# A decoder trunk in split float32 on one core: the operands of each stage at distances of their own from a multiple of 2048 bytes

## The reference

```python
mem_n = rmsnorm(mem, mem_norm)
for i in range(2):
    x = x + 0.5 * swiglu_ffn(rmsnorm(x, ffn1_norm[i]), ffn1_w_in[i], ffn1_w_out[i])   # 1024 -> 2*2816 -> 1024
    h = rmsnorm(x, mix_norm[i])
    mk, mv = split(mem_n @ mem_w_kv[i])
    z = h @ w_in[i]                                # hgrn: 1024 -> 5120; gmlp: 1024 -> 5120
    x = x + concatenate([mixer(z), memory_attention(z, mk, mv)]) @ w_out[i]
    x = x + 0.5 * swiglu_ffn(rmsnorm(x, ffn2_norm[i]), ffn2_w_in[i], ffn2_w_out[i])
return rmsnorm(x, final_norm)
```

## Time and profile before

| | before |
|---|---|
| median of 3 runs | 2362.61 us (2361.79 to 2364.54) |
| profiled execution, its own time | 2362.44 us |
| its span | 2360.7 us |
| TensorE busy, matmuls | 2340.6 us, 99% |
| VectorE busy | 1197.9 us, 51% |
| ScalarE busy | 743.0 us, 31% |
| GpSimd busy | 263.3 us, 11% |
| mean DMA rate | 99 GB/s |

### The profile page before, as it was taken

One profiled execution on the slowest core, in us unless ns is written; L12 is line 12 of the kernel. 1 busy time (PEld: TensorE's weight loads), 2 busy tenths in 40 slices (PEclk: granted clock), 3 DMA queues, 4 the chain that ended last, 5 costly groups with the idle time before them and its releaser, 6 DMA issues.

```text
span 2360.7 us, 29488 instructions
## 1 busy us (share of the span) xinstructions
PE 2340.6 (99%) x10944; PEld 1943.6 (82%) x10944; DVE 1197.9 (51%) x1411; ACT 743.0 (31%) x1005; POOL 263.3 (11%) x235
## 2 busy tenths in 40 slices
PE   9999999999999999999999999999999999999998
PEld 9988888877888888888878888887788888888887
DVE  6654443446888654444445444344337644444422
ACT  4432222234444322222223223123333322322322
POOL 3400001111333420000110000120001212000000
PEclk9999999999999999999999999999999999999999
DMA  7733333332222333333333333333233233333322
GB/s 233 215 98 96 94 94 98 98 107 63 72 71 78 100 91 97 98 98 98 97 90 91 96 98 98 98 98 98 70 94 88 83 96 107 98 98 94 93 95 92
DMA packets 400691, 234.32 MB, mean 99 GB/s; under 512 B 7692, under 2 KB 386672, under 8 KB 400624
## 3 DMA queue, kind: packets, MB, share of 16 engines
q1 hardware_dynamic: 397328, 223.37, 32.1%
q0 software_dynamic: 3280, 10.02, 1.2%
q10 hardware_dynamic: 16, 0.00, 0.0%
HBM read 227.07 MB, written 6.29 MB: 99 GB/s over the span
## 4 chain that ended last, share of the span: by engine, by line
PE 95%; DVE 2%; ACT 1%; issue 1%; DMA 0%; POOL 0%; ACTq 0%; DVEq 0%; SPq 0%; POOLq 0%
PE acc L1012 26%; PE acc L1014 26%; PE acc L1013 26%; PE acc L766 1%; PE acc L768 1%; PE acc L767 1%; PE mix L398 1%; PE mix L385 1%; PE acc L249 1%; PE acc L251 1%; PE acc L250 1%; PE mix L250 1%; PE mix L249 1%; PE mix L251 1%; PE mix L833 1%
## 5 line engine op out<-in xcount | busy, mean ns | idle before, releaser
L1174 DVE TENSOR_TENSOR w_lo<-raw,w_hi 128x1024 fp32r<-128x1024 f32 (+1 forms) x422 | 548.3, 1302 | 658.4 <-ACT w_hi L1444 647.8
L1012 PE MATMUL acc<-h_hi,w_hi 128*128 128x512 f32 x1920 | 759.2, 395 | 7.5 <-DVE h_lo L1236 5.3
L1014 PE MATMUL acc<-h_hi,w_lo 128*128 128x512 f32 x1920 | 748.4, 390 | 0.0
L1013 PE MATMUL acc<-h_lo,w_hi 128*128 128x512 f32 x1920 | 747.9, 390 | 0.0
L1444 ACT ACTIVATE w_hi<-raw 128x1024 fp32r<-128x1024 f32 (+1 forms) x422 | 436.5, 1038 | 354.3 <-DMA raw<-in_ffn_w_out_dram 222.0
L1012 PEld LDWEIGHTS acc<-h_hi,w_hi 128*128 128x128 f32 x1920 | 361.3, 188 | 85.2 <-DVE h_lo L1236 6.6
L1013 PEld LDWEIGHTS acc<-h_lo,w_hi 128*128 128x128 f32 x1920 | 361.2, 188 | 77.0 <-issue 3.7
L1014 PEld LDWEIGHTS acc<-h_hi,w_lo 128*128 128x128 f32 x1920 | 360.9, 188 | 75.6
L1012 PE MATMUL acc<-act_hi,w_hi 128*128 128x512 f32 (+1 forms) x976 | 368.7, 378 | 2.6 <-DVE act_lo L1185 1.7
L1014 PE MATMUL acc<-act_hi,w_lo 128*128 128x512 f32 (+1 forms) x976 | 366.2, 375 | 0.0
L1013 PE MATMUL acc<-act_lo,w_hi 128*128 128x512 f32 (+1 forms) x976 | 366.1, 375 | 0.0
(11 more groups left out here) (214 smaller groups left out, 1779.0 us busy)
## 6 DMA issues: line engine op xcount, KB each, us to landing
raw<-in_ffn_w_in_dram SPq DMA_DIRECT2D x176, 512.0 KB, 3.7
raw<-in_ffn_w_out_dram SPq DMA_DIRECT2D x70, 512.0 KB, 4.0
raw<-in_hgrn_w_in_dram SPq DMA_DIRECT2D x40, 512.0 KB, 3.7
raw<-in_gmlp_w_in_dram SPq DMA_DIRECT2D x40, 512.0 KB, 3.6
raw<-in_mem_w_kv_dram SPq DMA_DIRECT2D x32, 512.0 KB, 4.2
raw<-in_gmlp_w_out_dram SPq DMA_DIRECT2D x24, 512.0 KB, 4.0
raw<-in_ffn_w_out_dram SPq DMA_DIRECT2D x24, 384.0 KB, 3.4
raw<-in_hgrn_w_out_dram SPq DMA_DIRECT2D x16, 512.0 KB, 4.0
```

The lines of the kernel that those rows point to most:

```text
L1012: pe.matmul(bank, w_hi[:, j, i, :], hi, start=(start and i == 0), stop=False)
L1013: pe.matmul(bank, w_hi[:, j, i, :], lo, start=False, stop=False)
L1014: m = pe.matmul(bank, w_lo[:, j, i, :], hi, start=False, stop=(stop and i == last))
L1174: dve.tensor_tensor(w_lo[:, j, 0:nkb], raw[:, j, 0:nkb], f32(w_hi[:, j, 0:nkb]), ALU.subtract).then_inc(w_lo_ready, 1)
```

## The change

The halves of h are now views of one tile, `h_flat`, with 2048 bytes to spare, and each `_in` stage s has two numbers of elements (4 bytes each) in `H_AT[s]`, by which its h_hi and h_lo begin behind a multiple of 2048 bytes: (512, 512), (0, 0), (64, 64), (0, 64), (1024, 1024), (128, 128) bytes for s = 0 to 5. The activations of the four feed-forward parts have `ACT_AT[n_ffn]`: (64, 64), (256, 256), (0, 1024), (0, 0) bytes; they use two spare blocks of act_hi and act_lo. The mixer's activations and the memory's halves stay where they were. act_hi, act_lo, work and vecs begin 2048 bytes later than before.

```diff
+H_ROOM = 512
+H_AT = [(128, 128), (0, 0), (16, 16), (0, 16), (256, 256), (32, 32)]
+ACT_AT = [(16, 16), (64, 64), (0, 256), (0, 0)]
...
-        with nc.sbuf_tensor("h_hi", [P, DB, T], F32R) as h_hi, nc.sbuf_tensor("h_lo", [P, DB, T], F32R) as h_lo:
+        with nc.sbuf_tensor("h_flat", [P, 2 * DB * T + H_ROOM], F32R) as h_flat:
             pass
-        out_rows = sb("out_rows", [P, 2 * DB, T])[:, 0:DB, :].rearrange("p b t -> p (b t)").rearrange(
-            "p (tb c) -> p tb c", tb=TB)
+        out_rows = sb("out_rows", [P, 2 * DB * T + H_ROOM])[:, 0:DB * T].rearrange("p (tb c) -> p tb c", tb=TB)
+
+        def h_views(s):
+
+            hi, lo = H_AT[s]
+            return [h_flat[:, at:at + DB * T].rearrange("p (b t) -> p b t", t=T) for at in (hi, DB * T + lo)]
...
+        def act_views(n):
+
+            hi, lo = ACT_AT[n]
+            return [part[:].rearrange("p b t -> p (b t)")[:, at:at + FB * T].rearrange("p (b t) -> p b t", t=T)
+                    for part, at in ((act_hi, hi), (act_lo, lo))]
...
-                unit(ph.q0 + it, j, h_parts, acc[j][:], True, True, each if first and j == 0 else None)
+                unit(ph.q0 + it, j, h_parts_of(s), acc[j][:], True, True, each if first and j == 0 else None)
...
+                    top, rest = act_views(n_ffn) if kind == "ffn_out" else (act_hi, act_lo)
...
-                            parts = [(act_hi[:, a0 + k, :], act_lo[:, a0 + k, :]) for k in range(nkb)]
+                            parts = [(top[:, a0 + k, :], rest[:, a0 + k, :]) for k in range(nkb)]
...
-                            dve.tensor_tensor(act_lo[:, f, :], tmp[:, j, :], f32(act_hi[:, f, :]),
+                            dve.tensor_tensor(rest[:, f, :], tmp[:, j, :], f32(top[:, f, :]),
...
-                act.activation(h_hi[:, m_, :], t, ACT.Copy).then_inc(h_hi_ready, 1)
+                act.activation(h_views(s)[0][:, m_, :], t, ACT.Copy).then_inc(h_hi_ready, 1)
```

More of the change, by code:

```diff
@@ L754, in v_tensor @@
                 pe.wait_ge(w_lo_ready, LANES * q + j + 1)
+                h_hi, h_lo = h_views(4)
                 top = w_hi[:, j].rearrange("p (k z) c -> p k (z c)", k=2)
@@ L1064, in _, with h_parts_of @@
                 (k_quad if kind == "k" else v_quad)(it)
-            h_parts = [(h_hi[:, k, :], h_lo[:, k, :]) for k in range(DB)]
+            def h_parts_of(s):
+                hi, lo = h_views(s)
+                return [(hi[:, k, :], lo[:, k, :]) for k in range(DB)]
             def in_unit(ph, s, it, j, first=False):
@@ L1119, in u_unit @@
                             pe.wait_ge(acc_read, ph.g0 + 2 * XH + LANES * it + j - 3)
-                        unit(ph.q0 + 6 + it, j, h_parts, acc[j][:], True, True)
+                        unit(ph.q0 + 6 + it, j, h_parts_of(s), acc[j][:], True, True)
                     for j in range(LANES):
@@ L1234, in h_rest @@
             def h_rest(s, m_, t):
+                h_hi, h_lo = h_views(s)
                 dve.wait_ge(h_hi_ready, DB * s + m_ + 1)
@@ L1305, in up, with low @@
                             dve.tensor_tensor(tmp[:, j, :], tmp[:, j, :], tmp[:, j - 1, :], ALU.mult).then_inc(prod_done, 1)
-                        def rest(j):
+                        def low(j):
                             f = 2 * it + j // 2
+                            top, rest = act_views(n_ffn)
                             dve.wait_ge(act_hi_ready, f0 + j // 2 + 1)
-                            dve.tensor_tensor(act_lo[:, f, :], tmp[:, j, :], f32(act_hi[:, f, :]),
+                            dve.tensor_tensor(rest[:, f, :], tmp[:, j, :], f32(top[:, f, :]),
                                               ALU.subtract).then_inc(act_lo_ready, 1)
@@ L1318, in body @@
                         lo(ph.q0 + it + 1, 0)
-                        rest(1)
+                        low(1)
                         gate(2)
@@ L1322, in body @@
                         up(3)
-                        rest(3)
+                        low(3)
                     body(0, first=True)
@@ L1515, in top @@
                             act.wait_ge(prod_done, f0 + j // 2 + 1)
-                            act.activation(act_hi[:, 2 * it + j // 2, :], tmp[:, j, :], ACT.Copy).then_inc(act_hi_ready, 1)
+                            act.activation(act_views(n_ffn)[0][:, 2 * it + j // 2, :], tmp[:, j, :], ACT.Copy).then_inc(act_hi_ready, 1)
                         hi(ph.q0 + it, 2)
```

## The result

The changed kernel takes 2374.18 us (median of 5 runs, 2373.63 to 2376.05); the kernel before, beside it, 2363.27. The ratio is 1.0049, with a 95% interval from 1.0034 to 1.0064: slower, by 10.9 us.

A forecast was written before the change was run, and what follows sets the result against it. TensorE was taken as the bound, busy 2340.6 of 2360.7 us, with 512-column matmuls starting every 226.7 ns. All six terms were put at 0, so the forecast stayed at 2362.6 us, range 2356 to 2372.

The forecast's parts named there:

- seam: Fixed cost of 13.3 ns paid by each TensorE matmul whatever its length, beside 106.7 ns per 256 columns streamed.
- Step 1: Third ffn_in loop: one more VectorE register instruction, 10 repeats, some 0.5 us, hidden by idle waits; cost 0.
- Step 2: ScalarE's and VectorE's writes of h and act halves to shifted places: 0.2 us at worst or gained, taken as 0.
- rival D: VectorE or ScalarE slower on shifted tiles: 2363 us, inside the forecast and counted in its 78%.
- Step 3: 2048 bytes more for h: tiles behind it move by a whole 2048 bytes, no distance changes; 0.
- Step 4: Streamed operands off a multiple of 2048, 5328 matmuls of 512 columns: 0 per matmul, bounded by -71 to +71 us.
- the nearest rows: Trace rows of even pitch across 1024-byte memory-part steps, 512-byte weight steps, and h against act; grounds for 0 per matmul.
- The bounds of -13.3 and +13.3 ns: Price limits per shifted streamed matmul: the fixed cost vanishes, or running over a 2048 multiple adds another.
- Step 5: Stationary h in the v part of s = 4, 384 matmuls at 1024 bytes more: slices only trade distances; 0.
- Step 6: Stage starts: waits unmoved; half-clock losses may come or go, +-1.7 us for each of a few starts; 0 added.
- Rival A: TensorE streams running over a 2048 multiple need a second fetch, 5328 matmuls: slower, 2434 us at full price; 13%.
- Rival B: Fixed matmul cost is an address clash of two reads that shifted places would part: faster, 2292 us full price; 9%.

## Why the prediction was wrong

- **What bounds the kernel** held: TensorE's pitch was the whole story, and a tenth of a nanosecond did cost 0.9 us. The pitch of 226.7 and the seam of 13.3 ns were read rightly.
- **Step 1**, the register instruction, held: it is there nine times at 40 ns (ten at 53 were forecast), and VectorE still waits 53.8 us for acc and 54.0 for w_hi in that stretch.
- **Step 2**, the writes, held, and so rival D has no part in the result: waits for h_lo are 5.3 us in both profiles, and an h_lo subtraction takes 746 ns in the median in both.
- **Step 3** held, by the kernel with multiples of 256 (ratio 1.0004).
- **Step 4 failed**, in two places. The first is the count. I took 5328 matmuls as shifted because their operands left a multiple of 2048; by the runs only a difference modulo 256 to the weights counts, which leaves s = 2, 3 and 5 and n = 0, 3696 matmuls, and of s = 3 all, not the third whose operand moved. The second is the price: 0 where the traces show 2.25 ns at (64, 64), 5.3 at (0, 64), 5.7 at (128, 128). What misled me is in the sentences on the nearest rows. The weights' places 0, 512, 1024, 1536 and the memory part's 0 and 1024 looked like a sweep of distances with an even pitch. All of them are multiples of 256: it was one distance, seen many times. Three nearby rows that agree are one row if they share the period. The bounds of -13.3 and +13.3 ns held for every kernel (the most was +11.2, at 4 bytes); the value of 0 within them had no support for distances of 64 and 128. The prediction's own sign of being wrong, a shifted stage with another pitch, came true in four stages.
- **Step 5** was right for the wrong reason: the v part stayed at 226.9 because 1024 is a multiple of 256. At 192 it went to 229.0, so stationary slices do not merely trade distances.
- **Step 6** held: two stretches of half clock became none, worth 3.4 us in the spans, and it hid a fifth of the bill in the profiled execution.
- **Rival A** had the sign, and at a tenth of a seam a time (2370) 4 us short, but its mechanism is refuted: it named s = 0 as slow, which kept its pitch, and (0, 64) as a third of the price, where it cost 5.3 ns against 2.25 for (64, 64).
- **Rival B**, that the place decides by where two reads meet, was closer in mechanism than A and had the sign wrong. If that is the mechanism, the kernel before already sat where the reads meet least. Of the 13.3 ns that remain no difference took anything away at 512 columns. The 216 ns that the Trainium skill ("TensorE: Matmul & The Clock Gate", section "Back-to-back issue gap") gives for an isolated matmul was reached in none of the stages read here, where the least is 226.7.

What is shown: the pitch is 226.7 ns (226.9 in the v part) wherever the streamed and the loaded operand begin at the same place modulo 256 bytes, wherever that place is; at every other difference tried it is 228.9 ns or more, and the loss is TensorE's own, with every other engine and the DMA idle. That its two reads clash in the memory is the likely picture, and only argued. Open is which reads, why the price is 64 < 16 < 128 < 32, and why 128 and (64, 0) have more than one.

## What to carry to other kernels

Where TensorE's pitch is the bound and matmuls are like these (fp32r, 512 columns, a new load for each), let the streamed and the stationary tiles begin at the same place modulo 256 bytes; multiples of 2048 are not needed. A small tile of odd size ahead of them in the allocation can shift one against the other and cost up to 11 ns of a 227 ns matmul (4 bytes), or 1.9% of this kernel (192 bytes everywhere), while TensorE's busy share stays at 99%. Count matmuls in a window of one shape to see it, and before taking rows as a sweep of some quantity, ask by which period they could all be the same.

## What the runs showed of the hardware that was not expected

- The period of 256 bytes, the dependence on the difference, and that a pure change of place costs 2 to 11 ns of 226.7.
- For blocks of 256 columns a difference can **help**. In the memory part of the kernel with the weights at 64 bytes, 11 starts lie 1.25 us apart, 114 ns each, where the earlier trace rows have 120:

```profile
84.94 0.28 PE L1071 MATMUL acc<-w_hi,act_hi 128*128 128x256 f32 x1
...
86.19 0.28 PE L1073 MATMUL acc<-w_hi,act_lo 128*128 128x256 f32 x1
```

 The seam is thus not a constant of the engine. Not every gap is so short: over the whole memory part the mean is 115.3 ns where the weights are loaded and 117.5 where they are streamed, against 119.8 and 119.9 before; in the other kernel with the weights at 64 bytes it is 116.0 and 116.1, and with the weights at 128 it is 118.7 and 119.0. It brought this kernel little: the first ffn_in started at 111.5 in place of 112.1 us, and no run tells whether these 0.6 us come from it.
- Every matmul's record is lengthened with its pitch only a little (the median of L1027 is 392 ns after, 389 before), and the loads stay at 188 ns. The loss can't be read from the loads' rows.
